# A float32 decoder layer on one core: where the activation buffers begin in the on-chip memory, modulo 512 bytes

## The chip, the core and the metric

The kernel runs on one core of a Trainium2 chip. The core has five engines that run side by side: TensorE (matrix products; PE, with its weight loads shown apart as PEld), VectorE (DVE), ScalarE (ACT), GpSimd (POOL) and SyncE (SP, which here only issues DMAs). Their shared on-chip memory has 128 partitions; a buffer takes the same byte range in each of them, so a buffer has one start address, counted in bytes within a partition. The metric is the time of the program on the device in microseconds (us), the median of several executions; lower is better.

## The reference, cut to what matters

One decoder layer for 256 tokens of width 2048, all in float32. It begins with an input projection, two attention branches (dilated windows, and latent attention), gates, an output projection and a layer norm. Then comes a layer of 16384 small experts of which 128 are picked per token, and a second layer norm:

```python
proj = h @ w_in[l]                              # queries, keys, values, latents, gates
y_a = y_a @ a_w_out[l];  y_b = y_b @ mla_w_out[l]
mix = (g_a * y_a + g_b * y_b) @ w_out[l]
h = layer_norm(ALPHA * h + mix, ln1_g[l], ln1_b[l])
# peer: every expert is computed as  gelu(expert_down @ h), then gate * that @ expert_up
y_p = peer(h, peer_w_query[l], sub_keys_1, sub_keys_2, expert_down[l], expert_up[l])
h = layer_norm(ALPHA * h + y_p, ln2_g[l], ln2_b[l])
```

## The kernel before, in words

All the weights come from one DRAM tensor, `stream`, as 425 tiles of 128 x 2048 float32 (1 MB), each in two halves of 128 x 1024. SP brings a half into one of four slots of `raw`. ScalarE rounds it to `w_hi` (L349), VectorE writes the rest, `raw - w_hi`, to `w_lo` (L603), and TensorE uses both. An activation is held in the same way, as a `_hi` and a `_lo` buffer. So every product of the layer is three matmuls: `w_hi` with the high part, `w_hi` with the low part, `w_lo` with the high part (`three`, ending in the matmul of L974).

In the order of time the tiles are:

- 64 tiles for the first attention's queries, keys, values and gates, 9 for the latents, 16 for the second gates. They multiply `a_hi` and `a_lo`.
- 16 pairs for the heads of the latent attention. The first tile of a pair (`up_proj`) multiplies `c_hi` and `c_lo`, the second `b_hi` and `b_lo`.
- 16 tiles with `a_hi`, `a_lo` (the output projection of the second branch), 16 with `b_hi`, `b_lo` (`w_out`), 16 with `a_hi`, `a_lo` (the expert queries).
- 128 tiles `T_DN` (`expert_down`) with `a_hi`, `a_lo`. During the first 48 of them VectorE also picks the experts: a unit of that work (one of eight heads, one of two token blocks; 16 units) is spread over three tiles, between the calls that write `w_lo`. These 48 tiles are a loop of two passes with 24 tiles and 8 units each.
- 128 tiles `T_UP` (`expert_up`), where the roles are turned: the activation `m_hi` or `m_lo` is loaded as the stationary operand and 512 columns of `w_hi` or `w_lo` are streamed (`up`, L1170).

In all other tiles the stationary operand (loaded by LDWEIGHTS, 128 columns) is a 512-byte piece of `w_hi` or `w_lo`, and the moving operand is 256 columns, 1024 bytes, of the activation. One tile is 48 such pairs of a weight load and a matmul, or in `T_UP` 24 pairs with 512 columns.

Each engine works its instructions off in the order written, and semaphores tie the engines together: `lo_ready` lets TensorE use a half, `half_used` lets ScalarE overwrite it, `acc_free` hands the accumulators back.

**Where the buffers lie.** `sb` takes memory in the order of the calls. The first buffer, `raw`, begins at byte 16512, which is 128 modulo 512. `raw`, `w_hi`, `w_lo`, `a_hi`, `a_lo` and `res` have 16384 bytes each, so all six begin at 128 modulo 512. Then come `cst` (8832 bytes, that is 128 more), `small` (320), `stat` (64) and `carrier` (64). So `b_hi`, which follows, begins at 128 + 128 + 448 = 704, that is at 192 modulo 512. All large buffers after it have sizes that are multiples of 512 bytes: `b_hi`, `b_lo`, the gates, `c_hi`, `c_lo` and `head` lie at 192. So do `h1_n`, `qp`, `m_hi` and `m_lo`, which reuse the memory from the same start. Rows and slices that the matmuls take are multiples of 512 bytes apart, so a buffer's start gives the residue of every operand cut from it.

Of the kernel before, what the change touches and what calls it, by code (L numbers as in the profile page):

```python
# [31 lines left out]
P = 128  # L32
# [51 lines left out]
N_SMALL = 4 * KD + 2 * KL + 8  # L84
# [44 lines left out]
def build(nc, stream, x_t, const_in, small_in, keys_t, ln2, y_out, a_dram, g_dram):  # L129
    ctx = ExitStack()  # L130

    def sb(name, shape, dt=F32, stack=ctx):
        return stack.enter_context(nc.sbuf_tensor(name, shape, dt))
# [5 lines left out]
    raw = sb("raw", [P, 4, HALF])  # L139
    w_hi = sb("w_hi", [P, 4, HALF], F32R)  # L140
    w_lo = sb("w_lo", [P, 4, HALF], F32R)
    a_hi = sb("a_hi", [P, KD, T], F32R)
    a_lo = sb("a_lo", [P, KD, T], F32R)
    res = sb("res", [P, KD, T])
    cst = sb("cst", [P, N_CONST])
    small = sb("small", [P, N_SMALL])
    stat = sb("stat", [P, 16])
    carrier = sb("carrier", [P, 16])

    mix_mem = ExitStack()  # L150
    b_hi = sb("b_hi", [P, KD, T], F32R, mix_mem)
# [1135 lines left out]
```

## Time and profile before

| | |
|---|---|
| time, median of 3 runs | 2586.66 us (2585.81 to 2590.33) |
| time of the profiled execution | 2591.99 us |
| its span, first to last instruction | 2590.3 us |
| TensorE busy | 2548.9 us, 98% of the span |
| VectorE, ScalarE, GpSimd busy | 1463.4, 1161.1, 548.7 us |
| mean DMA rate | 201 GB/s |

TensorE's share says how long at least one matmul was in flight, not how fast they follow each other: a matmul is shown with a duration of 280 ns or so, while the next begins some 120 ns after it. The distance from start to start, here called the pitch, is what the kernel's time is made of. It is read from a stretch in which the engine never pauses, as the length of the stretch over the number of matmuls in it.

### The profile page before, as it was taken

How to read it: one execution, taken by the hardware profiler on the slowest of the kernel's cores; microseconds unless marked ns; L12 is line 12 of the kernel's file. 1: busy time of each engine (PE TensorE's matmuls, PEld its weight loads, DVE VectorE, ACT ScalarE, POOL GpSimd, SP SyncE). 2: the span in 40 equal slices, each digit the busy share in tenths (PEclk: the TensorE clock that was granted, in tenths of full speed). 3: DMA queues.
4: the chain of work that ended last, by engine and by line, in shares of the span. 5: the costliest groups of instructions: out<-in, count | busy, mean ns of one | idle time of the engine just before them, and what ended most of it. 6: DMA issues, size and time to landing. Idle time of an engine off the chain costs nothing.

```text
span 2590.3 us, 49776 instructions
## 1 busy us (share of the span) xinstructions
PE 2548.9 (98%) x17963; PEld 2383.3 (92%) x17964; DVE 1463.4 (56%) x2391; ACT 1161.1 (45%) x1626; POOL 548.7 (21%) x377
## 2 busy tenths in 40 slices
PE   8999999999999998999999999999999999999997
PEld 8999999999999997999999999999988888888886
DVE  5455554445656655469897444444455555555556
ACT  4444444444444433465655343344444444444444
POOL 0000000000000002038888888800000000000000
PEclk9999999999999997999999999999999999999999
DMA  7666665454444553557787877776666767766664
GB/s 259 216 211 215 203 210 191 167 172 149 134 151 159 191 181 130 178 157 203 202 203 208 202 206 203 210 237 205 207 234 236 235 235 235 237 235 233 230 232 145
DMA packets 179838, 521.11 MB, mean 201 GB/s; under 512 B 52768, under 2 KB 52768, under 8 KB 179536
## 3 DMA queue, kind: packets, MB, share of 16 engines
q1 hardware_dynamic: 124128, 449.89, 53.5%
q0 software_dynamic: 51056, 53.89, 9.5%
q10 hardware_dynamic: 4608, 16.78, 1.6%
q8 instruction: 21, 0.34, 0.1%
q14 instruction: 25, 0.20, 0.0%
HBM read 484.70 MB, written 35.78 MB: 201 GB/s over the span
## 4 chain that ended last, share of the span: by engine, by line
PE 92%; DVE 5%; issue 2%; ACT 1%; DMA 0%; DVEq 0%; ACTq 0%; SPq 0%
PE ps L974 60%; PE ps L1170 27%; DVE w_lo L603 1%; PE ps L1013 1%; PE ps L1015 1%; PE ps L1028 1%; PE ps L1021 0%; PE ps L1124 0%; PE ps L1139 0%; ACT w_hi L349 0%; PE ps L1029 0%; PE ps L1008 0%; DVE idx L817 0%; DVE a_lo L783 0%; DVE idx L808 0%
## 5 line engine op out<-in xcount | busy, mean ns | idle before, releaser
L603 DVE TENSOR_TENSOR w_lo<-raw,w_hi 128x1024 fp32r<-128x1024 f32 x850 | 1015.3, 1223 | 849.4 <-ACT w_hi L349 830.0
L974 PE MATMUL ps<-a_hi,w_hi 128*128 128x256 f32 x3984 | 1143.0, 287 | 21.6 <-DVE w_lo L603 17.0
L974 PE MATMUL ps<-a_lo,w_hi 128*128 128x256 f32 x3984 | 1132.5, 284 | 0.0
L974 PE MATMUL ps<-a_hi,w_lo 128*128 128x256 f32 x3984 | 1132.4, 284 | 0.0
L349 ACT ACTIVATE w_hi<-raw 128x1024 fp32r<-128x1024 f32 x850 | 866.0, 1053 | 273.7 <-PE ps L1170 191.8
L974 PEld LDWEIGHTS ps<-a_hi,w_hi 128*128 128x128 f32 x3984 | 768.6, 193 | 27.3 <-issue 16.8
L974 PEld LDWEIGHTS ps<-a_lo,w_hi 128*128 128x128 f32 x3984 | 769.2, 193 | 0.5
L974 PEld LDWEIGHTS ps<-a_hi,w_lo 128*128 128x128 f32 x3984 | 769.0, 193 | 0.0
L320 POOL DMA_INDIRECT g_dram<-gate_v,where x256 | 462.4, 1806 | 199.6 <-DVE gate_v L854 119.0
L1170 PE MATMUL ps<-w_hi,m_hi 128*128 128x512 f32 x1008 | 317.1, 396 | 0.0
L1170 PE MATMUL ps<-w_hi,m_lo 128*128 128x512 f32 x1008 | 316.9, 396 | 0.0
L1170 PE MATMUL ps<-w_lo,m_hi 128*128 128x512 f32 x1008 | 316.9, 396 | 0.0
L1170 PEld LDWEIGHTS ps<-w_hi,m_hi 128*128 128x128 f32 x1008 | 189.5, 188 | 45.7
L1170 PEld LDWEIGHTS ps<-w_hi,m_lo 128*128 128x128 f32 x1008 | 189.5, 188 | 45.7
L1170 PEld LDWEIGHTS ps<-w_lo,m_hi 128*128 128x128 f32 x1008 | 189.5, 188 | 45.7
L533 ACT ACTIVATE act<-ps 128x256 f32<-128x256 f32 x128 | 49.3, 385 | 360.1 <-PE ps L974 354.7
L310 POOL DMA_DIRECT2D a_in<-a_dram x32 | 17.0, 533 | 802.4 <-DVE m_f L881 798.7
L527 ACT ACTIVATE m_hi<-m_f 128x256 fp32r<-128x256 f32 x128 | 53.6, 419 | 208.6 <-DVE m_f L881 208.6
L974 PE MATMUL ps<-b_hi,w_hi 128*128 128x256 f32 x512 | 144.4, 282 | 0.0
L974 PE MATMUL ps<-b_lo,w_hi 128*128 128x256 f32 x512 | 143.1, 279 | 0.0
L974 PE MATMUL ps<-b_hi,w_lo 128*128 128x256 f32 x512 | 142.9, 279 | 0.0
L302 POOL TENSOR_SCALAR res<-res,small 128x256 f32<-128x256 f32 x16 | 18.0, 1139 | 584.2 <-DVE a_lo L783 584.2
(170 smaller groups left out, 1705.3 us busy)
## 6 DMA issues: line engine op xcount, KB each, us to landing
raw<-stream SPq DMA_DIRECT2D x850, 512.0 KB
g_dram<-blank POOLq DMA_DIRECT2D x32, 512.0 KB, 6.2
a_dram<-act ACTq DMA_DIRECT2D x32, 512.0 KB
a_in<-a_dram POOLq DMA_DIRECT2D x32, 512.0 KB, 5.2
g_in<-g_dram POOLq DMA_DIRECT2D x32, 512.0 KB, 6.5
g_dram<-gate_v,where POOLq DMA_INDIRECT x256
res<-x_t SPq DMA_DIRECT2D x4, 512.0 KB, 6.8
ln_s<-ln POOLq DMA_DIRECT2D x1, 2048.0 KB, 11.3
```

Source lines behind the costliest of these rows:

```text
L302: ins = pool.tensor_scalar(res[:, k, :], res[:, k, :], small[:, S_B1 + k:S_B1 + k + 1], None, ALU.add)
L310: pool.dma_start(a_in[:, b], a_dram[i * 2 + b]).then_inc(ag_in[b], 16)
L320: pool.indirect_dma_start(out=g_cell, out_offset=bass.IndirectOffsetOnAxis(ap=where[:, tt, k:k + 1], axis=0), in_=gate_v[:, tt, k:k + 1], ...
L349: act.activation(w_hi[:, t.slot(hf), :], raw[:, t.slot(hf), :], ACT.Copy).then_inc(hi_ready, 1)
L527: act.activation(m_hi[:, par, :], m_f[:, par, :], ACT.Copy).then_inc(mhi_ready, 1)
L533: act.activation(act4[:, b // 4, b % 4, :], acc[t.par][:, 0:T], ACT.Gelu).then_inc(acc_free[t.par], 1)
L603: dve.tensor_tensor(w_lo[:, s, :], raw[:, s, :], w_hi[:, s, :].bitcast(F32), ALU.subtract).then_inc(lo_ready, 1)
L974: ins = pe.matmul(out, w, a, start=first and q == 0, stop=last and q == 2)
L1013: ins = pe.matmul(ps_s[:, o:o + k1], q_s[:, q0:q0 + P], k_s[:, 0:k1], start=True, stop=not rope)
L1015: ins = pe.matmul(ps_s[:, o:o + k1], qr_s[:, q0:q0 + P], kr_s[:, 0:k1], start=False, stop=True)
L1028: pe.matmul(ps_o[:, 0:T], v_s[:, 0, :], p_t[:, 0:T], start=True, stop=False, skip_group_check=True)
L1170: ins = pe.matmul(ps[:, o:o + 512], m[:, b % 2, s], w[:, t.slot(hf), 512 * c:512 * c + 512], start=False, stop=False, skip_group_check=True)
```

## The change

Three small buffers that are declared after `cst` (`small`, `stat`, `carrier`, together 448 bytes) are declared ahead of `a_hi`, and an unused buffer of 96 float32 (384 bytes) is declared after `cst`. No instruction is added, removed or moved; only addresses differ.

```diff
     w_lo = sb("w_lo", [P, 4, HALF], F32R)
+    small = sb("small", [P, N_SMALL])
+    stat = sb("stat", [P, 16])
+    carrier = sb("carrier", [P, 16])
     a_hi = sb("a_hi", [P, KD, T], F32R)
     a_lo = sb("a_lo", [P, KD, T], F32R)
     res = sb("res", [P, KD, T])
     cst = sb("cst", [P, N_CONST])
-    small = sb("small", [P, N_SMALL])
-    stat = sb("stat", [P, 16])
-    carrier = sb("carrier", [P, 16])
+    sb("gap_b", [P, 96])
 
     mix_mem = ExitStack()
     b_hi = sb("b_hi", [P, KD, T], F32R, mix_mem)
```

| start modulo 512 | before | after |
|---|---|---|
| `raw`, `w_hi`, `w_lo` | 128 | 128 |
| `a_hi`, `a_lo`, `res`, `cst` | 128 | 64 |
| `b_*`, `c_*`, `head`, `p_t`, `m_*` and all later large ones | 192 | 64 |

## Rows read from the trace of the kernel before

**Rows 1.** The page: TensorE's line of part 1, then part 4.

```profile
PE 2548.9 (98%) x17963; PEld 2383.3 (92%) x17964; DVE 1463.4 (56%) x2391; ACT 1161.1 (45%) x1626; POOL 548.7 (21%) x377
...
PE 92%; DVE 5%; issue 2%; ACT 1%; DMA 0%; DVEq 0%; ACTq 0%; SPq 0%
```

**Rows 2.** TensorE by stretch: us, busy (instructions), granted clock, DMA share, GB/s.

```profile
802.00:892.00 90.00, 90.00 (x753) 1.00 0.56 180
898.00:975.00 77.00, 77.00 (x656) 1.00 0.60 190
1300.00:1840.00 540.00, 540.00 (x4502) 1.00 0.76 210
1900.00:2500.00 600.00, 600.00 (x2573) 1.00 0.69 234
```

**Rows 3.** Groups by line and form: count | busy us, mean ns | idle before.

```profile
L974 PE MATMUL ps<-a_hi,w_hi 128*128 128x256 f32 x3984 | 1143.0, 287 | 21.6 <-DVE w_lo L603 17.0 <-DVE a_lo L783 4.5
...
L974 PEld LDWEIGHTS ps<-a_lo,w_hi 128*128 128x128 f32 x3984 | 769.2, 193 | 0.5
...
L1170 PE MATMUL ps<-w_hi,m_hi 128*128 128x512 f32 x1008 | 317.1, 396 | 0.0
...
L1170 PEld LDWEIGHTS ps<-w_hi,m_hi 128*128 128x128 f32 x1008 | 189.5, 188 | 45.7
L974 PE MATMUL ps<-b_hi,w_hi 128*128 128x256 f32 x512 | 144.4, 282 | 0.0
...
L974 PEld LDWEIGHTS ps<-b_hi,w_hi 128*128 128x128 f32 x512 | 96.2, 188 | 0.0
...
L974 PE MATMUL ps<-c_lo,w_hi 128*128 128x256 f32 x256 | 71.4, 279 | 0.0
```

**Rows 4.** The chain of waits, whole: pieces of one tile each (start us, us, what).

```profile
28.73 5.76 PE ps L974 x48
...
581.35 5.66 PE ps L974 x48
```

**Rows 5.** The timeline of VectorE, around one unit and the loop's end.

```profile
1221.82 2.36 DVE L603 TENSOR_TENSOR w_lo<-raw,w_hi 128x1024 fp32r<-128x1024 f32 x2
...
1239.01 2.36 DVE L603 TENSOR_TENSOR w_lo<-raw,w_hi 128x1024 fp32r<-128x1024 f32 x2
...
1255.78 0.28 DVE L854 TENSOR_SCALAR gate_v<-val,stat 128x16 f32 x1
1260.52 2.36 DVE L603 TENSOR_TENSOR w_lo<-raw,w_hi 128x1024 fp32r<-128x1024 f32 x2 [4.46 <-issue]
```

**Rows 6.** The chain of waits in the same stretch.

```profile
1114.45 23.05 PE ps L974 x192
...
1256.22 4.16 issue
1260.52 1.24 DVE w_lo L603
```

**Rows 7.** TensorE's waits from 1236 to 1300: total us, times, longest.

```profile
PE ps L974 <- DVE w_lo L603: 3.4, 1, 3.4
```

**Rows 8.** Groups by line: small matmuls against `cst`, and one among the `head` buffers.

```profile
L1021 PE MATMUL ps<-cst,logit 128*128 128x128 f32 x96 | 15.8, 273 | 0.4 <-DVE logit L630 0.4
...
L1008 PE MATMUL ps<-cst,v_t 128*128 128x128 f32 x64 | 12.2, 272 | 0.0
...
L1124 PE MATMUL ps<-gate_a,cst 128*128 128x256 f32 x32 | 9.5, 470 | 2.9 <-ACT gate_a L503 2.9
...
L1065 PE MATMUL ps<-head,cst 128*128 128x256 f32 x16 | 3.8, 379 | 0.0
```

**Rows 9.** The page: the largest group of VectorE and of ScalarE.

```profile
L603 DVE TENSOR_TENSOR w_lo<-raw,w_hi 128x1024 fp32r<-128x1024 f32 x850 | 1015.3, 1223 | 849.4 <-ACT w_hi L349 830.0
...
L349 ACT ACTIVATE w_hi<-raw 128x1024 fp32r<-128x1024 f32 x850 | 866.0, 1053 | 273.7 <-PE ps L1170 191.8
```

## The prediction, written before the changed kernel was run

> **What bounds the kernel now.** I read the page's busy shares first, then the chain of waits, then TensorE by stretch, and last the groups by form. TensorE is busy for 98% of the span, and the chain that ended last runs through it for 92% [rows 1]. VectorE and ScalarE mostly wait: the largest group of each has hundreds of us of idle time before it, ended by ScalarE and by TensorE [rows 9]. The DMA engines are busy for 0.56 to 0.76 of the time in the long stretches [rows 2], so the stream of weights keeps up. The time is therefore the number of matmuls times their pitch, and a change that touches only addresses can act almost only through that pitch.
>
> So the next view is the pitch, stage by stage, in stretches where TensorE never pauses [rows 2]. About two of the matmuls that a stretch counts only reach into it from its edges.
> - `a_hi`, `a_lo`: 90.00 us / 751 = 119.8 ns, and 540.00 / 4500 = 120.0 ns.
> - `b_hi`, `b_lo`: 77.00 us / 654 = 117.7 ns.
> - `T_UP`, 512 columns: 600.00 / 2571 = 233.4 ns.
>
> The chain says the same for single tiles: 5.76 us for 48 matmuls is 120.0 ns in the `a` tiles, 5.66 us is 117.9 ns in a `b` tile of the latent heads [rows 4]. I take 117.8 for `b`. The groups by form agree over all executions of the line: a `b` matmul lasts 282 ns and a `c` one 279, where an `a` one lasts 287, and a weight load lasts 188 against 193 ns [rows 3].
>
> These matmuls have the same line, shape, type and code around them. The first two stretches follow each other directly and see nearly the same DMA traffic (180 and 190 GB/s) and clock (1.00) [rows 2]. What differs is the buffer. `a_*` begins at the same residue as the weights, 128, so moving minus stationary is 0; `b_*` and `c_*` begin at 192, so it is +64. That a coincidence of the two streams costs 2.2 ns per matmul is the reading that I take; other differences between the buffers, their absolute place above all, are not excluded.
>
> **The change part by part.** It adds no instruction and no wait; it moves operands.
>
> *`a` tiles, 0 to -64.* There are 64 + 9 + 16 + 16 + 16 + 128 = 249 tiles of 48 matmuls, 11952 in all, which is three times the 3984 of one group [rows 3]. The trace has no 256-column matmul whose moving operand lies 64 below its stationary one. It has one with 512 columns: in `T_UP` the moving `w` (128) lies 64 below the stationary `m` (192). There the weight load takes 188 ns, as in the `b` tiles and not as in the `a` tiles [rows 3], and half its pitch is 116.7 ns. So I take the -64 place to be free of the coincidence too, with the pitch of the nearest rows of the same form: 117.8 instead of 120.0, -2.2 ns. The bounds are 116.7 (half of `T_UP`'s, below) and 122.2 (the same 2.2 ns on the wrong side, above).
>
> *Not all of these tiles can give it.* In the first 48 `T_DN` tiles VectorE has its picking to do. One of its units starts at 1221.82 and the next at 1239.01 [rows 5]: 17.19 us for three tiles, against 3 x 5.76 = 17.28 us on TensorE. At the end of the first pass VectorE stands for 4.46 us with nothing to wait for [rows 5], TensorE runs dry and waits 3.4 us for `w_lo` [rows 7], and the chain leaves TensorE 23.05 us into the pass and goes through VectorE up to 1260.52 [rows 6]. So the first pass is set by VectorE, and its 24 tiles give nothing. The second pass starts with TensorE and VectorE level. TensorE would want 3 x 48 x 117.8 = 16.96 us per unit, but gets 17.19: it gives 8 x (17.28 - 17.19) = 0.7 us instead of 2.5. That leaves 249 - 48 = 201 tiles: 201 x 48 x 2.2 ns = 21.2 us, and 0.7: **-21.9 us**. Elsewhere VectorE needs two writes of `w_lo`, 2 x 1.22 = 2.4 us [rows 9], and one or two short operations per tile of 5.65 us, so it keeps its cover.
>
> *`b` and `c` tiles, +64 to -64.* 16 + 16 + 16 tiles are 2304 matmuls. With both sides equal they stay at 117.8: 0. Bounds: -1.1 ns each if they go to 116.7, -2.5 us; +2.2 ns if they fall to the `a` pitch, +5.1 us.
>
> *`T_UP`, -64 to +64.* 128 tiles are 3072 matmuls at 233.3 ns. By the same symmetry: 0. Bounds, from the pitch of the 256-column rows: if it now pays what the `a` matmuls pay, it loses up to 2 x 2.2 = 4.4 ns each, -13.7 us; if it gets twice the `a` pitch, 240.0 ns, it costs 6.7 ns each, +20.5 us. I take 0, the value nearest to the 188 ns of its weight loads.
>
> *Small matmuls against `cst`.* The transposes (96 and 64) and the sums with the ones (32, 16 and 4 more) [rows 8] go from a distance of 64 to a distance of 0, since `cst` and its partners are then all at 64. Some 212 matmuls times 2.2 ns is +0.5 us; the most, were it 2.2 ns for each 64 of their columns, is 2 us. Products within the `head` buffers keep their distance.
>
> *VectorE, ScalarE, DMAs.* `raw`, `w_hi` and `w_lo` stay, so the 850 writes of each (1223 and 1053 ns [rows 9]) read and write where they did. Evictions and norms move by 64 or 128 bytes beside a TensorE that is the bound; off the chain they cost nothing. The exception is the first pass of `T_DN`, where 1% on VectorE's 142 us would be 1.4 us, either way.
>
> Sum: -21.9 + 0 + 0 + 0.5 = -21.4 us. The profiled execution took 2591.99 us for a span of 2590.3, 5.3 us above the median; it would come to 2570.6. Against the median, 2586.66 - 21.4 = **2565 us**.
>
> A rule that speaks against this. The `b` tiles have the shorter pitch and the shorter weight load, which I put down to two reads of one memory. The Trainium skill, "SBUF — State Buffer", section "Who interferes with whom", gives TensorE two independent read ports, one for the moving operand and one for the weight load, and says that "PE and ACT never wait on anyone". By it the residues change nothing; the 2.2 ns between rows of one form are not explained by it.
>
> **The rivals.**
>
> *Addresses don't matter.* Then the `b` and `c` tiles are faster for another reason (they are other buffers, in other stages) and all stays: 2587. For it: only three places are seen, and each residue belongs to one set of buffers, so address and buffer can't be told apart. Against it: `b` and `c` agree though they feed different tile layouts, and the `a` pitch is 120 in stages as unlike as 802 to 892 and 1300 to 1840, with quite different work on VectorE.
>
> *Below is better than above.* If half of `T_UP`'s pitch is the true value at -64, the `a` matmuls gain 3.3 ns: 9648 x 3.3 = 31.8 and 0.7. The `b`, `c` tiles gain 2.5. But `T_UP` goes to +64 and takes twice 117.8 = 235.6, 2.3 ns more: +7.1. With 0.5 for the small ones: -27.4, 2559. Against it: a pitch may have a part that does not grow with the columns, so halving it says less than a row of the same form.
>
> *Only +64 helps.* The moving operand must lead the weight load; at -64 it lags and is met again. The `a` tiles stay at 120, the `b` and `c` tiles fall back to it: 5.1 us more, 2592.
>
> *-64 costs what +64 gives (the slower side).* The place is the read of the moving operand at each matmul. Lagging by 64 bytes it runs into the next weight load and loses 2.2 ns more than at 0, pitch 122.2. The first pass of `T_DN` hides 24 tiles (24 x 5.87 = 140.8 us, under the 147.4 us from 1114.45 to 1261.8). 225 x 48 x 2.2 = 23.8, `b` and `c` 2304 x 4.4 = 10.1, small ones 0.5: +34.4, 2621. The kernel gets slower as soon as the `a` pitch is over 120.0 with the `b` tiles back at it. For it: the only -64 row has another shape, and I can't subtract its fixed part. Against it: that row's weight loads take 188 ns.
>
> **How the numbers follow.** Forecast 0.50 (2565, its own range 2558 to 2572); below is better 0.14 (2559); no effect 0.12 (2587); only +64 helps 0.12 (2592); -64 costs 0.12 (2621). `T_UP`'s bounds, -13.7 and +20.5, lie on the forecast as 2551 and 2586. The range, 2550 to 2593, takes these and the first four cases and leaves out the last and some of the second's lower end. A measurement of this kernel can tell about 0.2%, 5.2 us. Faster: the first two, 0.64. Same: no effect and two thirds of the 2592 case, which lies on the border, 0.20. Slower: the rest, 0.16.
>
> **What would show it.** Right: the stretch of `T_DN` after the picking has a pitch near 117.8 (some 2549 matmuls in 300 us instead of 2500) and a weight load there 188 ns; `b` tiles keep 5.66 us; `T_UP` keeps 233.3; the first pass of `T_DN` is as long as before, some 147 us, and TensorE shows new waits for `w_lo` in the second. Wrong: an `a` pitch of 120.0 (no effect, or only +64 helps; the `b` tiles decide between the two), one above it, or a `T_UP` pitch that moves by more than 1 ns. A gain in the span with unchanged pitches would mean that I looked in the wrong place.

## The result and the profile after

The changed kernel takes 2507.19 us (median of 4 executions, 2506.46 to 2525.96) against 2588.49 us for the kernel before: the ratio is 0.9704, with a 95% interval of 0.9657 to 0.975. The forecast was 2565 us, with a range from 2550. The direction was right; the gain is 81 us where 21 were forecast, and the time lies outside the range.

The page of the changed kernel. TensorE's busy share is the same 98% as in [rows 1], so that share says nothing of the gain; the chain has moved a little to VectorE. All lines of the code are one number higher.

```profile
span 2504.8 us, 49777 instructions
PE 2459.9 (98%) x17964; PEld 2304.6 (92%) x17964; DVE 1463.4 (58%) x2391; ACT 1160.8 (46%) x1626; POOL 559.8 (22%) x377
...
PE 85%; DVE 10%; issue 4%; ACT 1%; DVEq 0%; DMA 0%; ACTq 0%; SPq 0%
```

TensorE by stretch, as in [rows 2]: the output projection (`a`), `w_out` (`b`), `T_DN` after the picking (`a`), and `T_UP`.

```profile
780.00:850.00 70.00, 70.00 (x620) 1.00 0.58 191
...
880.00:938.00 58.00, 58.00 (x514) 1.00 0.57 193
...
1400.00:1760.00 360.00, 360.00 (x3179) 1.00 0.78 223
1900.00:2400.00 500.00, 500.00 (x2186) 1.00 0.69 238
```

With two matmuls taken off for the edges: 360.00 us / 3177 = 113.3 ns where [rows 2] gave 120.0; 58.00 / 512 = 113.3 for `b` where they gave 117.7; 500.00 / 2184 = 228.9 where they gave 233.4. All three stages are faster, not one. The groups by line say it too, but more weakly. The `a` matmuls went from 287 to 282 ns and the `b` ones from 282 to 279 [rows 3], which is 5 and 3 ns where the pitch fell by 6.7 and 4.4: a matmul's duration is not its pitch and understates the change. The weight load of the `b` matmuls has the same 188 ns before and after, while their pitch fell by 4.4:

```profile
L975 PE MATMUL ps<-a_hi,w_hi 128*128 128x256 f32 x3984 | 1123.2, 282 | 25.0 <-DVE w_lo L604 20.3
...
L975 PE MATMUL ps<-b_hi,w_hi 128*128 128x256 f32 x512 | 142.9, 279 | 0.0
...
L975 PEld LDWEIGHTS ps<-b_hi,w_hi 128*128 128x128 f32 x512 | 96.2, 188 | 0.0
```

Where the 85.5 us of the two profiled spans (2590.3 to 2504.8) come from, read off the starts of each stage's first and last matmul; the stretch after the picking begins with its first tile, the 49th of `T_DN`:

| stage | before, us | after, us | difference | forecast |
|---|---|---|---|---|
| up to the latent heads (89 `a` tiles) | 561.6 | 538.4 | -23.2 | |
| output projection (16 `a`) | 93.8 | 88.9 | -4.9 | |
| expert queries (16 `a`) | 105.7 | 100.7 | -5.0 | |
| `T_DN` after the picking (80 `a`) | 463.1 | 438.2 | -24.9 | these four: -21.2 |
| `T_DN` with the picking (48 `a`) | 281.6 | 278.1 | -3.5 | -0.7 |
| latent heads and `w_out` (48 `b`, `c`) | 323.0 | 313.2 | -9.8 | 0 |
| `T_UP` | 717.9 | 704.4 | -13.5 | 0 |
| the rest | 43.6 | 42.9 | -0.7 | +0.5 |

### The profile page after: what moved, and what is told of

It reads as the page before. It is cut to its first block, busy times and chain, and to the rows that moved or that the text cites. A ratio compares the mean times of both kernels' runs of the same rounds, so it can differ in the third digit from the quotient of the medians.

```text
span 2504.8 us, 49777 instructions
## 1 busy us (share of the span) xinstructions
PE 2459.9 (98%) x17964; PEld 2304.6 (92%) x17964; DVE 1463.4 (58%) x2391; ACT 1160.8 (46%) x1626; POOL 559.8 (22%) x377
## 4 chain that ended last, share of the span: by engine, by line
PE 85%; DVE 10%; issue 4%; ACT 1%; DVEq 0%; DMA 0%; ACTq 0%
PE ps L975 53%; PE ps L1171 28%; DVE w_lo L604 3%; PE ps L1014 1%; DVE idx L818 1%; PE ps L1016 1%; DVE idx L809 1%; DVE work L810 1%; PE ps L1029 1%; DVE pick L844 0%; DVE pick L846 0%; DVE slot L848 0%; PE ps L1022 0%; PE ps L1125 0%; PE ps L1140 0%
## 5 line engine op out<-in xcount | busy, mean ns | idle before, releaser
L604 DVE TENSOR_TENSOR w_lo<-raw,w_hi 128x1024 fp32r<-128x1024 f32 x850 | 1015.4, 1223 | 779.7 <-ACT w_hi L350 770.4
L975 PE MATMUL ps<-a_hi,w_hi 128*128 128x256 f32 x3984 | 1123.2, 282 | 25.0 <-DVE w_lo L604 20.3
L975 PE MATMUL ps<-a_lo,w_hi 128*128 128x256 f32 x3984 | 1109.5, 278 | 0.0
L975 PE MATMUL ps<-a_hi,w_lo 128*128 128x256 f32 x3984 | 1109.3, 278 | 0.0
L975 PEld LDWEIGHTS ps<-a_hi,w_hi 128*128 128x128 f32 x3984 | 754.1, 189 | 34.1 <-issue 16.9
L975 PEld LDWEIGHTS ps<-a_hi,w_lo 128*128 128x128 f32 x3984 | 754.2, 189 | 0.0
L975 PEld LDWEIGHTS ps<-a_lo,w_hi 128*128 128x128 f32 x3984 | 753.8, 189 | 0.5
L321 POOL DMA_INDIRECT g_dram<-gate_v,where x256 | 473.5, 1849 | 192.2 <-DVE gate_v L855 114.0
L1171 PE MATMUL ps<-w_hi,m_lo 128*128 128x512 f32 x1008 | 311.6, 390 | 0.0
```

What stands on the lines that cost most here:

```text
L321: pool.indirect_dma_start(out=g_cell, out_offset=bass.IndirectOffsetOnAxis(ap=where[:, tt, k:k + 1], axis=0), in_=gate_v[:, tt, k:k + 1], ...
L604: dve.tensor_tensor(w_lo[:, s, :], raw[:, s, :], w_hi[:, s, :].bitcast(F32), ALU.subtract).then_inc(lo_ready, 1)
L975: ins = pe.matmul(out, w, a, start=first and q == 0, stop=last and q == 2)
L1171: ins = pe.matmul(ps[:, o:o + 512], m[:, b % 2, s], w[:, t.slot(hf), 512 * c:512 * c + 512], start=False, stop=False, skip_group_check=True)
```

## The experiments

Every kernel below is the kernel before with other gaps, and in three of them something more. "Distance" is the start of the moving operand minus that of the stationary one, modulo 512 bytes. Each fence has rows of TensorE by stretch: us, busy (number of instructions), granted clock, DMA share, GB/s. Two instructions are always taken off. The kernel before had medians of 2590.9 to 2592.1 us beside them.

### One residue for all, and a shift of everything

`e1_all_192` moves only `stat` to the front: all activations at 192. `e2_all_shifted` is the changed kernel with `sb("gap_r", [P, 16])` ahead of `raw`.

```diff
     w_lo = sb("w_lo", [P, 4, HALF], F32R)
+    stat = sb("stat", [P, 16])
     a_hi = sb("a_hi", [P, KD, T], F32R)
```

> Only stat (64 bytes) is declared ahead of a_hi: a_*, res and cst begin at 192 modulo 512, and b_*, c_*, m_* stay at 192; weights at 128. All moving activations are at distance +64 of the weights. Distance theory (the pitch is a function of moving minus stationary address modulo 512): a matmuls take the b pitch of before, 117.8 ns, for 120.0; b, c 117.8, T_UP 233.3 unchanged; 11952 x 2.2 = 26 us less, minus what the first pass of T_DN hides, 2565 us. Symmetry theory of the prediction (any distance but 0 is as good): would now have to give 113.3 here too, 2517 us. Buffer theory (something else about a_* and b_* decides): a stays at 120.0, 2588 us.

> The changed kernel with 64 bytes in front of raw: everything moves up by 64, weights at 192, all activations at 128. Distances are those of the changed kernel (-64, and +64 in T_UP). Distance theory: pitches 113.3 and 228.9, 2507 us. Residue theory (the activation's own residue decides: 64 gives 113.3, 192 gives 117.8, 128 gives 120.0): a, b and c at 120.0, about 2590 us or more.

Measured: 2556.7 us (ratio 0.9867, 0.9838 to 0.9895) and 2511.2 us (0.9691, 0.9663 to 0.9719). `e2_all_shifted` has the pitches of the changed kernel:

```profile
880.00:930.00 50.00, 50.00 (x444) 1.00 0.59 193
...
1400.00:1760.00 360.00, 360.00 (x3179) 1.00 0.77 223
1900.00:2400.00 500.00, 500.00 (x2187) 1.00 0.69 237
```

So it is the distance that counts. Activations at 128 gave 120.0 ns with the weights at 128 and give 113.3 with the weights at 192; the residue theory falls. `e1_all_192` at distance +64 gives 360.00 / 3057 = 117.8 in `T_DN`, as the distance theory says:

```profile
1400.00:1760.00 360.00, 360.00 (x3059) 1.00 0.76 214
```

But its time is 8 us below the expectation, and the chain of waits shows why. In the latent heads the same distance runs a tile of 48 matmuls in 5.45 us, 113.5 ns each, where the kernel before had 5.66 us [rows 4] at the same addresses of `b_*` and `w_*`:

```profile
621.91 0.33 PE ps L1021 x3
622.24 5.45 PE ps L974 x48
```

From 90 us on the first attention does so too: three of every four tiles take 5.45 us and the fourth 5.66, the same way in head after head. One distance, one form of instruction, two steady pitches. That was in neither theory.

### Half of the change each

`e3_a_only` drops `gap_b` from the changed kernel (`a_*` at 64, the rest at 192); `e4_b_only` has `gap_b` alone (`a_*` at 128, the rest at 64).

> The changed kernel without gap_b: a_* at 64, b_*, c_*, m_* at 192 as in the kernel before. Distance theory: a 113.3 to 113.7 ns, b and c 117.8, T_UP 233.3. Against the changed kernel that is 2304 x 4.4 = 10.2 and 3072 x 4.4 = 13.7 us more: 2531 us. If the stages helped each other (one state of the whole program), b and T_UP would be fast here too, 2507 us.

> The kernel before with a gap of 384 bytes ahead of b_hi and nothing else: a_* at 128, b_*, c_*, m_* at 64. Distance theory: a 120.0, b and c 113.3, T_UP 228.9; against the kernel before 10.2 and 13.7 us less: 2564 us. This and e3_a_only should add up to the whole change (24 + 57 = 81 us).

Measured: 2531.0 us (0.9767, 0.9739 to 0.9796) and 2568.8 us (0.9914, 0.9885 to 0.9942). First `e3_a_only`, then `e4_b_only` (`b`, `T_DN`, `T_UP`):

```profile
880.00:930.00 50.00, 50.00 (x427) 1.00 0.55 182
...
1400.00:1760.00 360.00, 360.00 (x3179) 1.00 0.78 223
1900.00:2400.00 500.00, 500.00 (x2145) 1.00 0.69 234
```

```profile
880.00:930.00 50.00, 50.00 (x443) 1.00 0.60 194
...
1400.00:1760.00 360.00, 360.00 (x3003) 1.00 0.75 210
1900.00:2400.00 500.00, 500.00 (x2186) 1.00 0.70 239
```

`a` 113.3 with `b` 117.6 and `T_UP` 233.3; then `b` 113.4 with `a` 120.0 and `T_UP` 228.9. Each stage follows its own distance whatever the others do. The halves are 60 and 22 us below the kernel before on that chip, together 82, for 81 of the whole.

### A map of the distances

Four kernels with another distance in each stage. Their gaps are, in bytes, ahead of `a_hi` / after `cst` / ahead of `c_hi` / ahead of `m_hi`: `e5_map1` `small`, `stat` / 64 / 128 / 256; `e6_map2` 128, `stat`, `carrier` / 0 / 128 / 448; `e7_fine_below` 32, all three / 320 / 80 / 352; `e8_fine_above` 32 / 0 / 432 / 224. `e10_fine2`: 16, all three / 352 / 128 / 48. Small buffers that are not named here stay after `cst`, ahead of the gap.

> Another distance in each stage, weights at 128: a_* at 0 (distance -128), b_* at 256 (+128), c_* at 384 (256, half the period), m_* at 0 (moving minus stationary +128). So far: distance 0 gives 120.0, +64 gives 117.8 or 113.3, -64 mostly 113.3; T_UP at -64 233.3, at +64 228.9. Collision theory (the two reads disturb each other only when their 64-byte pieces coincide or follow closely): at +-128 and 256 the fast 113.3 in every stage, T_UP 228.9 or less; the time at or below the changed kernel's, 2500 to 2507 us. Ladder theory (the pitch depends on the whole phase of the two streams, with other slow places in the period): at least one of these three distances shows 117 ns or more.

> a_* at 384 (distance 256), b_* at 320 (+192), c_* at 448 (-192), m_* at 256 (-128 in T_UP). Collision theory: 113.3 in every stage and T_UP at 228.9 or below, 2500 to 2507 us. Ladder theory: 117 ns or more in at least one of them. c in e5 and a here have the same distance, 256, and must agree if only the distance counts.

> Distances finer than 64 bytes, below: a_* -32, b_* -96, c_* -16; T_UP 256. If memory is read in pieces of 64 bytes, -32 and -16 overlap the weights' piece and lie between the 120.0 of 0 and the 113.3 of -64 in level or equal one of them: a at 120.0 (2588 us) if any overlap is enough; a at 113.3 (2507 us) if a half-piece distance is already free. If the unit is 16 bytes, even c at -16 is at 113.3.

> Distances finer than 64 bytes, above: a_* +32, b_* +96, c_* +16; T_UP +192. Unit of 64 bytes: a and c at 117.8 to 120.0, b as at +64 or +128. Unit of 32 bytes or less: a as at +64, 117.8 for the most part with stretches of 113.3, 2557 us. T_UP at 228.9 if only closeness counts.

> Around the best place: a_* -48, b_* -80, c_* +48, T_UP +32. The map so far, period 256 bytes: 0 120.0, 16 116.9, 32 116.7, 64 117.8 or 113.3, 96 120.0, 128 118.7, -96 118.7, -64 113.3, -32 118.3, -16 119.7. If -64 is a point where two streams mesh exactly (unit 64 bytes), -48 and -80 are slower than 113.3; if it is the middle of a free region, they are at 113.3 and more steady. T_UP: 226.7 at 0, 228.9 at +64: +32 between them.

The distances finer than 32 bytes did not come about: buffers are placed at multiples of 32, as their addresses in the built programs show. The pitches agree with that: in the latent heads `c`, meant for -16 and +16, ran at 120.0 ns as at distance 0 and at 116.7 as `a` at +32. So `e7_fine_below` had `a` -32, `b` -96, `c` 0, `T_UP` 256; `e8_fine_above` had `a` +32, `b` +96, `c` +32, `T_UP` +192; `e10_fine2` had `a` -32, `b` -64, `c` +64, `T_UP` 0. Their times were 2582.0, 2587.9, 2556.4, 2564.3 and 2550.7 us, all slower than the changed kernel. Where these expectations name a pitch at 16 or -16, it was measured at another distance. The collision theory of `e5_map1` and `e6_map2` falls: farther apart is not better. Rows of `e5_map1` (`b` +128; `a` -128; `T_UP` +128), then `e6_map2` (`b` +192; `a` 256; `T_UP` -128):

```profile
880.00:930.00 50.00, 50.00 (x424) 1.00 0.60 194
...
1400.00:1760.00 360.00, 360.00 (x3036) 1.00 0.77 213
1900.00:2400.00 500.00, 500.00 (x2145) 1.00 0.70 234
```

```profile
900.00:950.00 50.00, 50.00 (x443) 1.00 0.60 195
1400.00:1760.00 360.00, 360.00 (x3002) 1.00 0.77 211
1900.00:2400.00 500.00, 500.00 (x2145) 1.00 0.70 234
```

`e7_fine_below` (`b` -96; `a` -32; `T_UP` 256) and `e8_fine_above` (`b` +96; `a` +32; `T_UP` +192):

```profile
880.00:930.00 50.00, 50.00 (x424) 1.00 0.61 191
...
1400.00:1760.00 360.00, 360.00 (x3045) 1.00 0.78 214
1900.00:2400.00 500.00, 500.00 (x2208) 1.00 0.71 241
```

```profile
900.00:950.00 50.00, 50.00 (x419) 1.00 0.58 188
1400.00:1760.00 360.00, 360.00 (x3088) 1.00 0.78 217
1900.00:2400.00 500.00, 500.00 (x2145) 1.00 0.70 234
```

And `e10_fine2`, with `b` at -64 but at the slower of its two pitches (50.00 / 425 = 117.6):

```profile
880.00:930.00 50.00, 50.00 (x427) 1.00 0.62 193
...
1900.00:2400.00 500.00, 500.00 (x2208) 1.00 0.72 241
```

Put together, the pitch in ns, with what most of the matmuls at a distance had (the `T_UP` places between were not tried):

| distance modulo 256 | 0 | 32 | 64 | 96 | 128 | 160 | 192 | 224 |
|---|---|---|---|---|---|---|---|---|
| 256 columns | 120.0 | 116.7 | 117.8 or 113.3 | 120.0 | 118.7 | 118.7 | 113.3 or 117.8 | 118.3 |
| `T_UP`, 512 columns | 226.7 | | 228.9 | | 233.3 | | 233.3 | |

The pattern repeats after 256 bytes, not 512: distances 0 and 256 give the same 120.0, +128 and -128 the same 118.7, +192 has the 113.3 of -64 in `w_out` (and 117.8 in the heads); in `T_UP` 0 and 256 give 226.7, -64 and +192 give 233.3. And the two forms want different distances: 0 is the worst place for 256 moving columns and the best for 512.

### Which reads meet

`e9_pairs` has `sb("gap_w", [P, 16])` ahead of `w_lo`, `small` and `stat` ahead of `a_hi`, and `sb("gap_al", [P, 16])` ahead of `a_lo`. `e15_a_lo` is the changed kernel with `a_lo` alone at distance 0 (`gap_al`, and `gap_b` 64 bytes shorter).

> Which weight load meets which matmul? w_hi at 128, w_lo at 192, a_hi at 64, a_lo at 128. The trio is (w_hi, a_hi), (w_hi, a_lo), (w_lo, a_hi). Next-load theory (a matmul's read runs beside the load for the matmul after it): the pairs are a_hi with w_hi, a_lo with w_lo, a_hi with w_hi, all at -64: a pitch 113.3, in the b and c stages a mixture. Own-load theory (only the distance to the matmul's own weights counts): -64, 0, -128, so a pitch well above 113.3, about the mean of 113.3, 120.0 and 118.7, 117.3 ns. Time by the first about 2530 us (b, c and T_UP not at their best), by the second some 40 us more.

> The changed kernel with a_lo alone moved by 64, to distance 0; a_hi stays at -64, and b_*, c_*, m_* at 64. Averaging theory (each matmul pays for its own distance): (113.3 + 120.0 + 113.3) / 3 = 115.6 ns in the a stages, 2507 + 11952 x 2.3 ns = some 2530 us. Whole-stream theory (the pitch comes from how the whole sequence of reads meshes, one misfit spoils it for all three): 117.8 ns or more, 2550 us or more.

Measured: 2572.9 us (0.9928, 0.9911 to 0.9945) and 2554.1 us (0.9856, 0.9838 to 0.9874). `w_out` and `T_DN` in `e9_pairs`, then the expert queries and `T_DN` in `e15_a_lo`:

```profile
884.00:969.00 85.00, 85.00 (x721) 1.00 0.60 190
...
1400.00:1760.00 360.00, 360.00 (x3039) 1.00 0.78 214
```

```profile
1010.00:1080.00 70.00, 70.00 (x596) 1.00 0.58 193
...
1400.00:1760.00 360.00, 360.00 (x3021) 1.00 0.75 212
```

360.00 / 3037 = 118.5 ns: the theory that only the load for the next matmul meets a matmul's read falls, since it wanted 113.3. The own-load theory wanted about 117.3 and is not hit either. 360.00 / 3019 = 119.2 ns in `e15_a_lo`, and 70.00 / 594 = 117.8 in its expert queries, where the mean of the three distances would be 115.6: the averaging theory falls, and here too one layout has two pitches. One operand out of step costs most of what all three cost. The pitch belongs to the whole sequence of reads and can't be added up from its matmuls.

The traces also say who takes part. In the `w_out` stage of `e9_pairs`, `b_hi`, `b_lo`, `w_hi` and `raw` begin where they do in `e6_map2`, and of the buffers that its matmuls read only `w_lo`, always the stationary operand there, begins 64 bytes higher: 85.00 / 719 = 118.2 ns against 50.00 / 441 = 113.4. So the place of the stationary operand matters by itself. And the other engines are not the cause: from 1400 to 1760 us of the kernel before, groups of three matmuls that begin while VectorE and ScalarE are both idle (320 of them) and while both work (186) have the same 120.0 ns; in the changed kernel it is 113.3 in both cases.

### The version from the map, and the changed kernel again

`e11_best` adds `sb("gap_m", [P, 16], F32, up_mem)` ahead of `m_hi` (distance 0 in `T_UP`). `e12_after` is the changed kernel.

> The changed kernel with 64 more bytes ahead of m_hi: m_* at 128, distance 0 in T_UP, where the map gives 226.7 instead of 228.9 ns; all else as in the changed kernel. Distance theory: 3072 x 2.2 = 6.8 us less than the changed kernel, 2500 us. If T_UP's fast place in the map came from something else in that layout (its place at 384), 2507 us.

> The changed kernel again, to compare with e11_best on one chip: 2507 us in most executions. One of its four executions so far took 2526 us. If the matmul stream has two steady pitches at -64, 113.3 and 117.8, and the last stretch of T_DN (some 3800 matmuls without a pause) can start in either, executions near 2507 + 17 = 2524 us turn up again now and then, and nothing between them and 2510.

Measured, in 6 and 7 executions: `e11_best` 2505.5 us (2501.6 to 2524.9; ratio 0.9691, 0.9664 to 0.9718), `e12_after` 2511.0 us (2507.6 to 2525.6; 0.9685, 0.9672 to 0.9697). `e11_best`, `T_DN` and `T_UP`:

```profile
1400.00:1760.00 360.00, 360.00 (x3179) 1.00 0.79 223
1900.00:2400.00 500.00, 500.00 (x2208) 1.00 0.72 241
```

`T_UP` runs at 226.6 ns, which over 3072 matmuls is the 6.8 us expected, and the lowest times, 2501.6 and 2507.6, lie 6.0 us apart. But the intervals overlap, and the totals of the two kernels are not told apart: both swing by more than that. The swing shows in the profiled execution of `e12_after`, which took 2522.5 us:

```profile
1400.00:1760.00 360.00, 360.00 (x3059) 1.00 0.76 215
1900.00:2400.00 500.00, 500.00 (x2186) 1.00 0.71 239
```

The same code at the same addresses: `T_DN` after the picking at 360.00 / 3057 = 117.8 ns throughout, where the changed kernel's trace had 113.3, and `T_UP` the same 228.9. 80 tiles x 48 x 4.4 ns = 16.9 us; the two profiled times are 16.0 apart. Contrary to what was expected of `e12_after`, two of its seven executions, at 2511.0 and 2513.8, lie between the groups. The weight loads tell the two traces apart as well: where the pitch is 117.8, one load in three takes 192 ns, and all three take 188 where it is 113.3:

```profile
L975 PEld LDWEIGHTS ps<-a_hi,w_hi 128*128 128x128 f32 x1019 | 195.6, 192 | 0.0
```

### Breaking the stream

`e13_kick` and `e14_kick_best` are `e12_after` and `e11_best` with

```diff
         with pe.Fori(0, NKEYS // 8) as i:
             for b in range(8):
+                if b == 0:
+                    for n in range(2):
+                        pe.transpose(ps_m[:, P * n:P * n + P], iota, ident)
                 full(Tile(T_DN + b, i, 8), a_hi, a_lo)
```

and one wait ahead of the loop for accumulators that are long free.

> The changed kernel with two small transposes (of a table, into an unused accumulator) ahead of every eighth T_DN tile. In e12 the 3840 matmuls after the picking ran at 117.8 ns in the profiled execution and at 113.3 in that of the changed kernel. If a stream keeps its pitch until something breaks it and chooses anew at each break (the heads of the first attention, where such transposes come with every head, are back at 113.3 each time), no execution can stay at 117.8 for more than eight tiles in a place where it does not belong: the times lie close together, 2509 to 2513 us (16 breaks of some 0.3 us added, of which the half in the picking is hidden), and none near 2523. If the pitch is fixed for an execution by something outside the stream, times near 2523 stay as frequent as in e12 (2 of 7).

> e11_best (m_* at distance 0) with the same transposes. By the first theory 2502 to 2507 us in every execution, where e11_best had 2501.6 to 2524.9; by the second the same spread as there.

Measured, in 5 executions of each: 2521.0 us (2519.7 to 2522.0; 0.9729, 0.9716 to 0.9743) and 2512.2 us (2507.4 to 2514.4; 0.9691, 0.9678 to 0.9705). Pieces between two breaks in `e13_kick`:

```profile
1360.00:1396.00 36.00, 36.00 (x320) 1.00 0.81 221
1400.00:1440.00 40.00, 40.00 (x342) 1.00 0.79 202
1445.00:1485.00 40.00, 40.00 (x356) 1.00 0.78 208
1490.00:1530.00 40.00, 40.00 (x342) 1.00 0.77 198
1580.00:1618.00 38.00, 38.00 (x338) 1.00 0.79 208
1625.00:1663.00 38.00, 38.00 (x325) 1.00 0.82 259
```

They are 113.2, 117.6, 113.0, 117.6, 113.1 and 117.6 ns (the piece from 1532 to 1575 is not in the list; it has 113.3). The breaks are at 1353, 1397, 1442, 1486, 1532, 1575, 1619 and on, and in this tail the pitch changes at them and nowhere between. So the stream keeps its pitch until it is broken and takes one anew at each break; nothing outside it holds for an execution. The break can be very small: in three places of the traces (`e14_kick_best` at 1271 us, `e15_a_lo` at 1188, `e8_fine_above` at 1230) the pitch changes at a delay of less than 20 ns, for which the profile shows no wait. The spread fell as expected, from 18 us to 2.3 in `e13_kick` (from 23 to 7 in `e14_kick_best`). The time did not: I expected each break to lead back to 113.3, and 4 of the 10 pieces of the tail took 117.8; the median is 10 us above that of `e12_after`. Nor is the choice a matter of chance alone. In the first attention of `e13_kick` every fourth tile ran at 117.8, in head after head, where the same code at the same buffer addresses had 113.3 throughout in `e12_after`. Two neighbouring tiles there, from the chain of waits:

```profile
225.29 5.66 PE ps L975 x48
231.27 5.46 PE ps L975 x48
```

What decides for one of the two at a break stays open.

## Why the prediction was wrong, step by step

**The bound and the method were right.** The kernel is its matmuls times their pitch. The change acted on nothing else: VectorE is busy for the same 1463.4 us, and its `w_lo` writes keep 1223 ns [rows 9].

**The residues matter, and by distance.** The reading of [rows 2] as an effect of addresses was argued there with a chance of 0.12 against it; `e2_all_shifted` and the two halves now show it. The Trainium skill, "SBUF — State Buffer", section "Who interferes with whom", lists for TensorE two independent read ports and has it wait for nobody. That section alone would have left the time as it was; these runs show a pitch between 113.3 and 120.0 ns by the distance of the two operands.

**The step that failed: "*`a` tiles, 0 to -64*", the value of -2.2 ns.** It took the 117.8 ns of the `b` rows as what a matmul costs with the coincidence gone. But 117.8 is only the slower of two pitches that +64 and -64 both have; the other is 113.3, and at -64 it prevailed. The term measures 6.7 ns, and 6.0 on the average over the four unhindered `a` stages (58.0 us over 9648 matmuls), because of the pieces at 117.8. The bound of 116.7 ns for it, half of `T_UP`'s pitch, was no bound. The two forms have their good places at different distances, so a row of one says nothing of the other at the same distance. The trace of before could not show 113.3: no stretch of it ran there.

**The same step again for `b`, `c` and `T_UP`.** Both were priced at 0 by symmetry, "with both sides equal". The sides are not equal: in the table, 64 and 192 share their two pitches for 256 columns, but with other frequencies, and for `T_UP` they differ outright, 228.9 and 233.3. They gave 9.8 and 13.5 us. `T_UP`'s lower bound of -13.7, got by supposing that it then paid what the `a` matmuls paid, was its value: 3072 x 4.4 ns, which is 13.5 and not 13.7. The weight load's 188 ns, used to choose 0, does not give the pitch: it is 188 at 228.9 as at 233.3.

**The picking was right in its mechanism.** Counted by TensorE's tiles, the first pass took 138.3 us before and 137.2 after, the second 143.3 and 140.9, together 3.5 us less for 48 tiles that would otherwise have given 15. The forecast was 0 and 0.7. VectorE's last instruction of the picking starts 284.1 us after the first matmul of `T_DN` before and 282.3 after: of these 1.8 us, 1.4 are the pause at the loop's end, 3.07 us instead of 4.46 [rows 5]. The other 1.7 us are TensorE running closer behind VectorE: its 49th tile starts 2.5 us ahead of that instruction before and 4.1 after. The forecast took the two as level and left this out. VectorE's timeline and TensorE's waits from 1060 to 1360, which are now eight:

```profile
1215.27 1.23 DVE L604 TENSOR_TENSOR w_lo<-raw,w_hi 128x1024 fp32r<-128x1024 f32 x1 [3.07 <-issue]
```

```profile
PE ps L975 <- DVE w_lo L604: 6.4, 8, 3.3
```

Each of these waits is also a break at which the stream may take the other pitch, the last of them at 1354, just ahead of the 430 us of the tail. The traces of the changed kernel and of `e12_after` part there: of the 16.0 us between them, this tail makes 16.9, the other stages together -0.9. That the slow executions without a trace part there too is likely, but not shown.

**The rivals.** "Below is better than above" had the right sign for the `a` stages and a size of 3.3 ns for 6.7; it had `T_UP` slower by 7.1 us where it got faster by 13.5. The others are refuted.

## What to carry to other kernels

When matmuls of one form run at different pitches in different stages, look at the distance between the start addresses of the moving and the stationary buffer before looking for a wait: here two shifts, of 448 bytes for the `a` buffers and of 384 for the rest, were worth 3% of a kernel that was 98% busy. Measure the map of distances, for each length of the moving operand by itself, and do not extend it by symmetry or from another length. One trace shows one of the steady pitches; take several executions before a stretch's pitch is used as a price.

## What the runs showed that I had not expected

- The pitch has a period of 256 bytes in the distance and is not monotonic: 113.3 to 120.0 ns for 256 float32 columns, 226.7 to 233.3 for 512.
- At distances of 64 and 192 the same stream has two steady pitches, 113.3 and 117.8 ns, keeps one over thousands of matmuls (3792 in the chain's longest piece) and changes where it is broken, if only by some 20 ns. Other layouts can have two as well: 119.2 and 117.8 in `e15_a_lo`.

The chain of the changed kernel shows that piece:

```profile
1354.59 430.06 PE ps L975 x3792
```

- That the moving operand and the stationary one disturb each other is shown by the buffers: moving either changes the pitch, and the other engines' work does not. How their reads meet is not shown: the experiments moved buffers and could not take the loads away, and `e9_pairs` rules out the simplest form. The places between 32 bytes, and the two operands of `T_UP` at odd multiples of 32, were not tried.
